# Strassen's scheme for the MLP's second product in a hybrid backbone block

## The reference, cut to what matters

```python
h = rmsnorm(x, norm2_g) * (1 + scale2) + shift2      # (2048, 1024)
a = h @ mlp_w1                                        # (2048, 4096)
a = jnp.square(jax.nn.relu(a))
x = x + gate2 * (a @ mlp_w2)                          # (2048, 1024)
out = rmsnorm(x, final_g)
```

## Time and profile before

| | |
|---|---|
| time, median of 3 runs | 2661.9 us (2660.89 to 2662.99) |
| profiled execution, first to last instruction | 2660.7 us |
| TensorE busy | 2524.6 us, 95% |
| VectorE busy | 1663.9 us, 63% |
| ScalarE busy | 988.4 us, 37% |
| second product, L2581 | 3072 matmuls |
| first product, L2518 | 2760 matmuls |
| low halves of the weights, L1955 | 171.2 us of VectorE |

### The profile page before, as it was taken

One profiled execution on the slowest core, in us unless ns is written; L12 is line 12 of the kernel. 1 busy time (PEld: TensorE's weight loads), 2 busy tenths in 40 slices (PEclk: granted clock), 3 DMA queues, 4 the chain that ended last, 5 costly groups with the idle time before them and its releaser, 6 DMA issues.

```text
span 2660.7 us, 37765 instructions
## 1 busy us (share of the span) xinstructions
PE 2524.6 (95%) x14972; PEld 1386.7 (52%) x14972; DVE 1663.9 (63%) x2892; ACT 988.4 (37%) x1920; POOL 409.8 (15%) x371
## 2 busy tenths in 40 slices
PE   7888999998899999989999999999999999999997
PEld 2444656654577958665544444444444444444443
DVE  6851545677776746465678777887865444454445
ACT  3844434458443424242544433332333122122212
POOL 1408446000000100031331111111010000000000
PEclk9999999999899999999999999999999999999999
DMA  7403222100100000041335434333346212212212
GB/s 232 135 25 123 98 91 84 22 28 8 29 17 18 10 26 10 34 112 37 76 121 176 143 107 151 119 129 129 123 155 236 79 53 87 87 46 85 87 60 64
DMA packets 146280, 229.70 MB, mean 86 GB/s; under 512 B 15225, under 2 KB 84857, under 8 KB 141481
## 3 DMA queue, kind: packets, MB, share of 16 engines
q1 hardware_dynamic: 141496, 210.52, 24.5%
q0 software_dynamic: 4608, 16.78, 1.9%
HBM read 163.97 MB, written 63.29 MB: 85 GB/s over the span
## 4 chain that ended last, share of the span: by engine, by line
PE 82%; DVE 7%; ACT 5%; issue 3%; DMA 1%; POOL 1%; SPq 0%; DVEq 0%; POOLq 0%; ACTq 0%
PE pb L2581 25%; PE pb L2518 22%; PE pb L329 13%; PE pb L338 4%; PE pb L2497 3%; PE pb L2447 2%; PE pb L2397 1%; PE pb L2124 1%; PE pb L2464 1%; PE pb L2465 1%; PE pb L295 1%; DVE arena L1603 1%; PE pb L2329 1%; PE pb L2413 1%; PE pb L2222 1%
## 5 line engine op out<-in xcount | busy, mean ns | idle before, releaser
L2581 PE MATMUL pb<-arena 128*128 128x512 f16 x3072 | 667.9, 379 | 0.0
L2518 PE MATMUL pb<-arena 128*128 128x512 f16 (+2 forms) x2760 | 590.0, 375 | 7.4 <-DVE arena L1955 4.1
L2581 PEld LDWEIGHTS pb<-arena 128*128 128x128 f16 x3072 | 300.6, 98 | 362.4
L2087 DVE SCALAR_TENSOR_TENSOR arena<-pb,arena 128x512 f32<-128x512 f32 x512 | 352.6, 691 | 183.7 <-PE pb L2581 183.1
L2518 PEld LDWEIGHTS pb<-arena 128*128 128x128 f16 x2760 | 267.9, 98 | 324.6 <-issue 5.7
L329 PE MATMUL pb<-arena 128*128 128x512 f16 (+1 forms) x1944 | 412.5, 374 | 12.3 <-DVE arena L1584 4.5
L329 PEld LDWEIGHTS pb<-arena 128*128 128x128 f16 x1944 | 191.3, 99 | 231.4 <-issue 19.4
L2062 DVE TENSOR_TENSOR arena<-arena,pb 128x512 f32<-128x512 f32 x224 | 149.4, 684 | 251.2 <-PE pb L2518 251.1
L1339 ACT ACTIVATE arena<-arena 128x512 f32<-128x512 f32 x256 | 160.3, 626 | 172.9 <-DVE arena L2062 168.9
L1339 ACT ACTIVATE arena<-pb 128x512 f32<-128x512 f32 x32 | 19.1, 596 | 511.1 <-PE pb L2518 510.3
L338 PE MATMUL pb<-arena 128*128 128x128 f16 x2880 | 172.8, 221 | 6.8 <-ACT arena L1119 4.9
(11 more groups left out here) (321 smaller groups left out, 3194.0 us busy)
## 6 DMA issues: line engine op xcount, KB each, us to landing
w1x<-arena SPq DMA_DIRECT2D x16, 1792.0 KB, 8.6
arena<-w1x SPq DMA_DIRECT2D x16, 1792.0 KB, 9.1
arena<-in_x SPq DMA_DIRECT2D x128, 128.0 KB, 4.1
arena<-in_ada_rest POOLq DMA_DIRECT2D x32, 512.0 KB, 3.9
arena<-in_mlp_w SPq DMA_DIRECT2D x64, 256.0 KB, 3.8
arena<-in_mlp_w SPq DMA_DIRECT2D x16, 1024.0 KB, 6.3
w2x<-arena SPq DMA_DIRECT2D x16, 1024.0 KB, 8.5
arena<-w2x SPq DMA_DIRECT2D x16, 1024.0 KB, 4.8
```

Source lines behind the costliest of these rows:

```text
L2087: dve.scalar_tensor_tensor(xs, pb[:, 4 + n % 4, :], 1.0 / (WS * AS), xs, ALU.mult, ALU.add).then_inc(S("acc"), 1)
L2518: mm = pe.matmul(pb[:, up_bank(g, j), c], W1P[g % 2][WDEST[a]][0][:, ws, P * k:P * k + P], token_op(b, L // 2, c)[:, k, hs, :], start=(k = ...
L2581: mm = pe.matmul(pb[:, 4 + n % 4, :], ACTP[sl][:, 2 * f + th, hs, P * tt:P * tt + P], W2P[sl][:, f, ws, BLK * dh:BLK * dh + BLK], start=(f ...
```

## The change

**Second product.** Two neighbouring sets are a pair, and the down steps of the first 14 sets become seven steps (`NSTEP`), each for one pair: Strassen's scheme in the same form, seven products of quadrants, each with 4 token tiles x 2 sets x 3 = 24 matmuls in four PSUM banks. A step has 28 blocks and 168 matmuls; two plain down steps had 32 and 192. The last two sets stay plain (`down_plain`). VectorE evicts each block into one of seven sums: four are quadrants of the residual stream, three are new (`acc1`, `acc6`, `acc7`); these are joined with the quadrants in the last step of a pass (`joined` on VectorE, `combine` on GpSimd), and before the first GpSimd subtracts one quadrant from another (`x_difference`).

**Order.** Up 0, up 1; then for each pair: up 2p+2, products 0 to 3 of step p, up 2p+3, products 4 to 6 of step p; then up 14, the whole last step, up 15, and the two plain sets.

**Activations.** The quadrants now stay in PSUM where they are squared (three of four), in banks chosen by `BANKS_LOW`; up needs seven operands per set in place of four, so VectorE makes four sums (`a_sum`) and seven low halves (`a_lo`), ScalarE seven high halves (`a_hi`). These stand between the evictions, at places given by tables (`A_SUMS`, `A_LO`). Those of sets 0 and 1 stand in ups 1 and 2.

**Weights.** W2 has seven operands per set: GpSimd still scales, VectorE makes four block sums (`w2_t1`, `w2_t2`) and seven low halves of 128 x 512, ScalarE seven high ones. W1's pieces have one buffer each instead of two. Operands of W2 and of the activations lie in 14 and 16 slots that are taken in turn (`slot_table`). Weights are kept and fetched piece by piece. At the passes' border half of the residual stream, parked in DRAM before pass 0 (`x_park`), is loaded after each stored tile, since both passes use the same SBUF place.

The core of the diff (VectorE, ScalarE, TensorE, SP):

```diff
         def steps():
-            out = [("U", 0)]
-            for s in range(1, NSET):
-                out += [("U", s), ("D", s - 1)]
-            return out + [("D", NSET - 1)]
+            out = [("U", 0, ()), ("U", 1, ())]
+            for p in range(NSTEP - 1):
+                out += [("U", 2 * p + 2, ()), ("D", p, (0, 1, 2, 3)), ("U", 2 * p + 3, ()), ("D", p, (4, 5, 6))]
+            out += [("U", STRASSEN, ()), ("D", NSTEP - 1, tuple(range(7))), ("U", NSET - 1, ())]
+            return out + [("C", STRASSEN, ()), ("C", NSET - 1, ())]
...
+        A_SUMS = {(0, 1): 0, (0, 3): 1, (1, 3): 2, (2, 3): 3, (4, 1): 0, (4, 3): 1, (5, 2): 2, (6, 1): 3}
+        A_LO = {(0, 2): (0,), (1, 0): (1,), (1, 1): (2,), (1, 2): (3,), (2, 0): (4,), (2, 2): (5,), (3, 1): (6,),
+                (4, 0): (0,), (4, 2): (1,), (5, 0): (2,), (5, 1): (3,), (5, 3): (4,), (6, 0): (5,), (6, 2): (6,)}
...
             def finals(pas):
                 for z in range(8 * pas, 8 * pas + 8):
                     sp.wait_ge(S("z_out"), z + 1)
                     store_tokens(sp, ORD[8 * (1 - pas) + z % 8], outb[z % 4], S(f"out_st{z % 4}"))
+                    if pas == 0:
+                        sp.dma_start(o_tile(z), dr["x_park"][:, D * z:D * z + D]).then_inc(late_sem("x_re"), 16)
...
             def act_up(pas, s):
...
+                for x in w2[0:3]:
+                    w2_hi(*x)
+                act.wait_ge(S("u_mm"), up_done(pas, s, 0))
...
+                a_copy(T0, pb[:, up_bank(pas, s, 0), :])
...
+                for x in w1[0:1]:
                     w_hi(*x)
+                act.wait_ge(S("u_c"), uc(pas, s, "A11"))
+                squared(pas, s, "A11", 0)
+                for x in w1[1:2]:
+                    w_hi(*x)
+                for x in w2[3:4]:
+                    w2_hi(*x)
+                for x in w1[2:4]:
+                    w_hi(*x)
+                act.wait_ge(S("u_c"), uc(pas, s, "A22"))
+                squared(pas, s, "A22", 1)
+                for x in w2[4:5]:
+                    w2_hi(*x)
+                for x in w1[4:5]:
+                    w_hi(*x)
+                act.wait_ge(S("u_c"), uc(pas, s, "A12"))
+                squared(pas, s, "A12", 2)
+                for x in w1[5:6]:
+                    w_hi(*x)
+                for x in w2[5:6]:
+                    w2_hi(*x)
+                act.wait_ge(S("u_c"), uc(pas, s, "A21"))
+                squared(pas, s, "A21", 3)
+                for x in w1[6:7]:
+                    w_hi(*x)
+                for x in w2[6:7]:
+                    w2_hi(*x)
...
             def dve_up(pas, s):
...
+                if w1:
+                    w1_q(s + 1)
+                if scheme:
+                    w2_t1(s - 1)
...
+                for x in w2[0:3]:
+                    w2_lo(*x)
+                if scheme:
+                    w2_t2(s - 1)
...
+                dve.tensor_tensor(bank(3), T0, bank(3), ALU.add).then_inc(S("u_c"), 1)        # A11
...
+                dve.tensor_tensor(T0, T0, bank(1), ALU.add).then_inc(S("u_c"), 1)             # U2
+                for x in w1[0:2]:
+                    w_lo(*x)
...
+                dve.tensor_tensor(TS, T0, bank(2), ALU.add).then_inc(S("u_c"), 1)             # U3
+                for x in w2[3:4]:
+                    w2_lo(*x)
+                for x in w1[2:3]:
+                    w_lo(*x)
+                    w1_r(s + 1)
+                    w1_p(s + 1)
...
+                dve.tensor_tensor(a22, TS, bank(4), ALU.add).then_inc(S("u_c"), 1)
+                dve.tensor_tensor(T0, T0, bank(4), ALU.add).then_inc(S("u_c"), 1)             # U4
+                for x in w1[3:4]:
+                    w_lo(*x)
+                for x in w2[4:5]:
+                    w2_lo(*x)
+                for x in w1[4:5]:
+                    w_lo(*x)
...
+                dve.tensor_tensor(a12, TS, bank(5), ALU.add).then_inc(S("u_c"), 1)
+                for x in w1[5:6]:
+                    w_lo(*x)
+                for x in w2[5:6]:
+                    w2_lo(*x)
...
+                dve.tensor_tensor(T1, T0, bank(6), ALU.add).then_inc(S("u_c"), 1)             # A21
+                for x in w1[6:7]:
+                    w_lo(*x)
+                for x in w2[6:7]:
+                    w2_lo(*x)
...
+            def bank_free(pas, s, j):
...
+                if j == 4:
+                    pe.wait_ge(S("u_act"), 9 * g + 1)
+                elif j in (5, 6):
+                    pe.wait_ge(S("u_c"), uc(pas, s, "U3" if j == 5 else "U4"))
...
+            def down_step(pas, p, qs):
+                for pos in qs:
+                    q = step_order(p)[pos]
+                    pe.wait_ge(S("s_lo"), SB["lo"] + op_base(pas, 2 * p + 1) + q + 1)
+                    for e in range(2):
+                        w2_there(pas, 2 * p + e, q)
+                    for tt in range(4):
+                        at = step_bank(pas, p, pos, tt)
+                        bank_evicted(pas, at)
+                        for e in range(2):
+                            left, right = act_slot(pas, 2 * p + e, q), w2_slot(pas, 2 * p + e, q)
+                            for m, (hs, ws) in enumerate(TERMS):
+                                mm = pe.matmul(pb[:, 4 + at % 4, :], left[:, hs, P * tt:P * tt + P], right[:, ws, :],
+                                               start=(e == 0 and m == 0), stop=(e == 1 and m == 2))
+                        mm.then_inc(S("d_mm"), 1)
```

More of the change, by code:

```diff
@@ new lines, in program, with up_bank, quadrant_bank, up_done @@
+        BANKS_LOW = (0, 2, 3, 1, 0, 3, 0)
+        def up_bank(pas, s, j):
+            if s == 0 and pas == 0:
+                return BANKS_FIRST[j]
+            return (BANKS_HIGH if s == 1 else BANKS_LOW)[j]
+        def quadrant_bank(pas, s, name):
+            if name == "A12" and s == 0 and pas == 0:
+                return up_bank(0, 0, 2)
+            return up_bank(pas, s, {"A11": 3, "A12": 5, "A22": 1}[name])
+        def up_done(pas, s, j):
+            g = NSET * pas + s
+            return 7 * g + ((1, 4, 4, 4, 5, 6, 7) if g == 0 else (1, 3, 4, 2, 5, 6, 7))[j]
@@ new lines, in uc, with w_count, w1_blocks @@
+        def uc(pas, s, name):
+            return 7 * (NSET * pas + s) + ("A11", "U2", "U3", "A22", "U4", "A12", "A21").index(name) + 1
+        WSEQ0 = (0, 4, 5, 1, 3, 2, 6)
+        WSEQ = (0, 1, 5, 4, 3, 2, 6)
+        W_PRODUCT = {a: j for j, (a, _) in enumerate(PRODUCTS)}
+        def w_count(s, op):
+            return 7 * s + (WSEQ if s else WSEQ0).index(op) + 1
+        SB = {"lo": 7 * NT // 2}
+        def w1_blocks(x):
+            if x == 0:
+                return [half_f32[:, 7 + i, 0:BLK].rearrange("p (a b) -> p a b", a=4) for i in range(4)]
+            return [view((48 if x == 2 else 64) + 2 * i, [4, P]) for i in range(4)]
@@ new lines, in dve_up @@
+                w2 = [(s - 1, q) for q in w2_order(s - 1)] if pas == 0 and s else []
+                bank = lambda j: pb[:, up_bank(pas, s, j), :]
+                a12, a22 = (pb[:, quadrant_bank(pas, s, name), :] for name in ("A12", "A22"))
+                scheme = w2 and s - 1 < STRASSEN
+                if w1:
+                    w1_q(s + 1)
+                if scheme:
+                    w2_t1(s - 1)
+                if s in (1, 2):
+                    a_sum(pas, s - 1, 0)
+                    a_lo(pas, s - 1, 0)
+                    a_sum(pas, s - 1, 1)
+                    for i in (1, 2, 3):
+                        a_lo(pas, s - 1, i)
+                    a_sum(pas, s - 1, 2)
+                    a_lo(pas, s - 1, 4)
+                    a_sum(pas, s - 1, 3)
+                    for i in (5, 6):
+                        a_lo(pas, s - 1, i)
```

759 lines of the change are left out of this document (510 added, 249 removed).

## The result

| | before | after |
|---|---|---|
| time, median | 2662.4 us (2660.9 to 2668.2, 4 runs) | 2690.1 us (2688.8 to 2691.9, 4 runs) |
| span of the profiled execution | 2660.7 us | 2687.6 us |
| TensorE busy | 2524.6 us, 95% | 2474.5 us, 92% |
| VectorE busy | 1663.9 us, 63% | 1790.9 us, 67% |

The ratio is 1.0098, with a 95% interval of 1.0085 to 1.011: slower by 0.85 to 1.1%. 2684 was predicted. The page of the changed kernel answers the earlier trace rows: TensorE's work fell by 50 us, and the chain that ended last now holds lines of VectorE and ScalarE.

The account below looks back on a forecast made before the run. It took TensorE to bound both passes before the change. Pass 0's +56.7 us and pass 1's -34.3 gave +22.4, a span of 2683.1; with 1.2 us around it, 2684 was predicted, slower, range 2650 to 2718.

Parts of the forecast that it names:

- Pass 1: Second pass: 36.3 us of matmuls saved, 2 us charged for up 1's late W1 fetches, -34.3 us.
- Gaps of VectorE: Pass 0 up steps: VectorE idles before weights' low halves, 1.95 us each at quadrants A12 and A21, 0.78 at A22.
- TensorE's stall: Pass 0: TensorE waits 2.7 us for a bank in every down part; addition U4 0.7 late in even ups.
- Order alone: Pass 0 cycle of two sets from the queues' program order, without further costs: 79.0 us, against 77.7 before.
- Lock and clock: Pass 0, per cycle: GpSimd's scaling stretching VectorE's instructions, 2.3 us, and TensorE's clock falling after stalls, 1.3.
- Start: From VectorE's first block sum at 1404.98 to up 3 of pass 0, said to begin at 1509.2.
- Up 13 to pass 1: End of pass 0, up 13 through the last step and plain sets; pass 1 said to begin at 2081.9.
- by counts it fits: Pass 0: VectorE's 108 instructions a cycle take 66.3 us beside TensorE's 72.5.
- TensorE stays bound: Rival, pass 0: ScalarE's conversions do not hold VectorE; cycle 72.5, time 2610; chance 0.08.
- the lock and the clock cost nothing: Rival, pass 0: GpSimd's stretching and clock falls are free; cycle 79.0, time 2656; chance 0.14.
- pass 1's weights come late: Rival, pass 1: weights cost 15 us in place of 2, some 5 more at later sets; 2702; chance 0.12.
- VectorE does not reach 0.605: Rival, pass 0: VectorE's instructions take 0.69 us each, 9.2 more a cycle; 2738; chance 0.11.

Follow-up runs that it names:

- conv_first: Changed kernel with ScalarE's high halves of weights moved ahead of the addition's wait and Relu and Square in pass 0's up steps: 2627.7 us.
- no_scale: Changed kernel with GpSimd multiplying only 8 columns of W2's block in place of 1024 in each instruction: 2673.1 us.
- start: Changed kernel with set 0's split W1 stored ahead of the two W2 loads, and set 3's W1 loaded after set 0's stores: 2682.4 us.
- lo_half: conv_first with VectorE writing the low halves of three of a set's seven activations twice in pass 0: 2646.7 us.

## Why the prediction was right

It said 2684, slower, by a chain through ScalarE in pass 0 that costs more than pass 1 gives; 2690.1 was measured. Taking the chain away (conv_first) turned the change into the gain it was made of. Step by step:

- **Matmuls.** 36.3 us a pass at 0.2158 each: pass 1's cycles took 72.52. Right.
- **Pass 1.** -36.3 + 2 = -34.3 was said, -32.5 measured. The late W1 cost 3.47 us, not 2. SP's queue was the cause, as said, the reloads in it too: issued 15.9 us behind the first matmul (15.2 was said), and TensorE began with the first piece 5.8 us later, where landing some 4 us on was said.
- **VectorE in pass 1.** 38.7 us hidden was said; 41.4 busy, hidden. Right.
- **Gaps of VectorE.** 1.95 at A12 and A21 and 0.78 at A22 were said; 1.79, 1.88 and 0.60 measured. Right in kind, 0.1 to 0.2 too large each (the working adds up to 1.90, and 1.95 was used).
- **TensorE's stall.** 2.7 us in each down part, and U4 0.7 late in even ups: 2.40, 2.63 and 0.77 to 1.17.
- **Order alone.** 79.0 us a cycle was said; the cycles of no_scale, without GpSimd's lock and with the clock at full, took 78.7. Right.
- **Lock and clock.** 2.3 + 1.3 = 3.6 was said; together 81.5 - 78.7 = 2.8. The clock's term was too large: it fell in six down parts of the five cycles, but only in the two long ones did a fall lengthen the cycle, by some 1.2 us each (24.97 and 24.99 us against 23.53 to 24.11), 0.5 a cycle; that the short ones would not pay, because VectorE is behind there, was said. That leaves 2.3 for the lock, as said. The parting is an estimate, since all six falls went with the scaling in no_scale.
- **Start.** The step that failed: 1404.98 to 1509.2, 104.2 us, was said, 115.6 measured. The keeps of set 0's W1 behind two 1 MB loads of W2, and set 3's load behind all of up 1's keeps, stood in the diff's SP code, and their queue was not laid out. With both moved (start) it is 102.5. GpSimd's part of it, 6 in the prediction, was 5.0 (no_scale).
- **Up 13 to pass 1.** 2081.9 - 1922.2 = 159.7 was said, 158.3 measured. Right.
- **Sum.** The start's 11.4 too few, less 1.7 that this execution was ahead at the first block sum, the cycles' 5.6 too many, 1.4 too many, pass 1's 1.8 too few: 4.5, and the span was 2687.6 where 2683.1 was said. That the errors of 11.4 and of 5.6 + 1.4 went opposite ways is luck; the sign is not, since the cycles of pass 0 alone (407.4 us against 5 x 77.7 = 388.5 before) and the start (115.6 us against some 94) outweigh the 32.5 that pass 1 gave.

**The rivals.** That TensorE stays bound was rejected for the order of the two queues; it was the right reason, since with another order it is bound. That the lock and the clock cost nothing: 2.8 a cycle. That pass 1's weights come late by 15 us: 3.47, and no second wait behind it. That VectorE does not reach 0.605: no_scale has it busy 66.8 us with 108 instructions, additions into PSUM among them, 0.618 each with those that stand alone at 0.69, so it very nearly does. The clause "by counts it fits", 66.3 of 72.5, was too easy: lo_half showed 1.8 us of room.

**The clock.** The windows of the changed kernel's down parts show the clock below full in 7 of 13: in four short ones, in two long ones and in the last step. One long part with a fall and one without, both with a stall of 2.63 us in them:

```profile
1656.68:1681.65 24.97, 22.34 (x98) 0.93 0.46 148
1738.82:1762.93 24.11, 21.22 (x97) 1.00 0.49 153
```

A fall in a short part costs nothing that can be seen. From the start of a short part to the start of the long one behind the next up it took 38.83 to 39.16 us with a fall (four times) and 39.42 without; where TensorE was not slowed, it stood longer for VectorE, which sets the pace there. One of each:

```profile
1617.68:1656.68 39.00, 35.67 (x157) 15.56 (x156) 33.72 (x53) 16.70 (x30) 5.53 (x2) 0.96 0.44 146
1781.06:1820.48 39.42, 34.33 (x157) 14.93 (x156) 34.13 (x53) 16.70 (x30) 5.11 (x2) 1.00 0.44 145
```

The Trainium skill, "TensorE: Matmul & The Clock Gate", section "A second HAM failure mode: psum-queue depth-cycling", has the clock go back and forth where matmul groups wait on cycling PSUM banks, and the prediction worked out from it that all 13 pay. The rows decide: about half had a fall, and three paid, the two long parts some 1.2 us each and the last step some 1.5 (40.74 us against 39.19 in start), 4 us of the 22.

## What to carry to other kernels

Where two engines hand work to each other in turn, each in program order, counting their busy time says little: lay out both queues with times, and look for an operand whose maker stands behind an unrelated dependent pair; moving it ahead of that wait was worth 62 us here, against 72.5 us of removed matmuls. Lay out the DMA queue in the same way: a transfer put later in a queue is paid by whatever stood behind its new place. And where a change gives an engine more work, add the stretching by its neighbour and the waits to the counted time before calling it hidden.
